# Two transformer blocks: odd attention's norms and scores beside its gate units, modulation blocks in other places of the load stream

## The reference

```
# odd layer: attention of 8 heads of 128, 2 key heads, over keys picked by an indexer
q, k, v, gate, qi, ki, wi = split(norm(x) @ od_w_in)
idx = sum_h wi[h] * relu(qi[h] @ ki.T / 8) + causal       # a row of scores for each query
keep = the 64 largest of each row of idx
logits = (rms(q) * gq) @ (rms(k) * gk).T / sqrt(128) + rel_bias + where(keep, 0, -1e30)
x = x + ((softmax(logits) @ v) * silu(gate)) @ od_w_out

# second block, layer i: six vectors of 1024 out of c, for x and for the context
mod = silu(c) @ ada_w[i] + ada_b[i]                       # 1024 x 6144 for each layer
sh1, sc1, g1, sh2, sc2, g2 = split(mod, 6)
h = rmsnorm(x) * g * (1 + sc1) + sh1
x = x + g1 * attention(h, context)
x = x + g2 * swiglu(rmsnorm(x) * g' * (1 + sc2) + sh2)
```

## Time and profile before

| | us |
|---|---|
| median of 3 runs | 1576.94 |
| lowest, highest | 1575.88, 1579.33 |
| profiled execution | 1575.75 |
| its span in the trace | 1574.0 |
| TensorE busy | 1484.5 (94%) |
| VectorE, ScalarE, GpSimd busy | 734.7, 598.3, 277.4 |
| last input unit of odd attention ends | 286.85 |
| output projection starts, ends | 349.63, 377.5 |

### The profile page before, as it was taken

One profiled execution on the slowest core, in us unless ns is written; L12 is line 12 of the kernel. 1 busy time (PEld: TensorE's weight loads), 2 busy tenths in 40 slices (PEclk: granted clock), 3 DMA queues, 4 the chain that ended last, 5 costly groups with the idle time before them and its releaser, 6 DMA issues.

```text
span 1574.0 us, 22641 instructions
## 1 busy us (share of the span) xinstructions
PE 1484.5 (94%) x9376; PEld 1251.6 (80%) x9376; DVE 734.7 (47%) x1204; ACT 598.3 (38%) x1130; POOL 277.4 (18%) x224
## 2 busy tenths in 40 slices
PE   7899999979999898999999998999999899999997
PEld 6878779847865586888888886688998678899997
DVE  6762145334349744323232234764454773255453
ACT  4434144244337625222122224442343461333342
POOL 2000187002000010211011111244500120021121
PEclk9899999899999998999999999999999999999999
DMA  7412464687200033313232232133351342646450
GB/s 230 164 55 85 160 245 139 252 332 279 81 27 1 28 107 143 125 58 139 85 107 74 95 120 112 54 108 107 114 192 44 107 162 107 267 171 211 168 174 28
DMA packets 36109, 206.84 MB, mean 131 GB/s; under 512 B 4952, under 2 KB 9480, under 8 KB 14888
## 3 DMA queue, kind: packets, MB, share of 16 engines
q1 hardware_dynamic: 33344, 200.11, 35.1%
q10 hardware_dynamic: 1848, 2.52, 0.8%
q0 software_dynamic: 816, 2.78, 0.5%
HBM read 202.76 MB, written 2.62 MB: 130 GB/s over the span
## 4 chain that ended last, share of the span: by engine, by line
PE 84%; DVE 7%; ACT 3%; DMA 3%; issue 1%; POOL 1%; SPq 1%; ACTq 0%; DVEq 0%; POOLq 0%
PE lin L1800 18%; PE lin L1802 17%; PE lin L1801 17%; PE lin L1767 4%; PE lin L1910 4%; PE lin L2381 4%; PE modp L1838 2%; DMA ring<-ada_in 2%; PE lin L2432 1%; PE lin L1783 1%; PE lin L1784 1%; PE lin L1785 1%; PE lin L2160 1%; PE aux L2302 1%; PE aux L1937 1%
## 5 line engine op out<-in xcount | busy, mean ns | idle before, releaser
L620 DVE TENSOR_TENSOR w_split<-ring,w_split 128x1024 fp32r<-128x1024 f32 (+1 forms) x140 | 187.5, 1344 | 358.7 <-ACT w_split L615 358.3
L615 ACT ACTIVATE w_split<-ring 128x1024 fp32r<-128x1024 f32 (+1 forms) x140 | 157.9, 1132 | 413.2 <-PE lin L1802 366.2
L1800 PE MATMUL lin<-hn_hi,w_split 128*128 128x512 f32 (+1 forms) x768 | 266.8, 347 | 3.5 <-DVE w_split L620 3.5
L1802 PE MATMUL lin<-hn_hi,w_split 128*128 128x512 f32 (+1 forms) x768 | 265.4, 346 | 0.0
L1801 PE MATMUL lin<-hn_lo,w_split 128*128 128x512 f32 (+1 forms) x728 | 249.9, 343 | 0.0
L1800 PEld LDWEIGHTS lin<-hn_hi,w_split 128*128 128x128 f32 x768 | 146.2, 190 | 21.1 <-issue 4.1
L1802 PEld LDWEIGHTS lin<-hn_hi,w_split 128*128 128x128 f32 x768 | 146.3, 190 | 17.5
L1801 PEld LDWEIGHTS lin<-hn_lo,w_split 128*128 128x128 f32 x728 | 138.7, 191 | 16.0 <-issue 0.5
L1801 PE MATMUL lin<-hid_split,w_split 128*128 128x512 f32 (+1 forms) x392 | 133.8, 341 | 0.0
L569 POOL TENSOR_TENSOR hn<-hn 128x256 f32<-128x256 f32 (+1 forms) x42 | 43.8, 1042 | 481.1 <-ACT hn L684 480.6
L1800 PE MATMUL lin<-hid_split,w_split 128*128 128x512 f32 (+1 forms) x352 | 118.5, 337 | 2.4 <-POOL hid_split L584 2.4
(11 more groups left out here) (435 smaller groups left out, 2978.7 us busy)
## 6 DMA issues: line engine op xcount, KB each, us to landing
ring<-ada_in SPq DMA_DIRECT2D x48, 1024.0 KB, 5.0
ring<-ssm_in_in SPq DMA_DIRECT2D x24, 1024.0 KB, 4.8
ring<-od_in_in SPq DMA_DIRECT2D x12, 1024.0 KB, 5.0
ring<-ffn0a_in_in SPq DMA_DIRECT2D x11, 1024.0 KB, 4.8
ring<-ffn0b_in_in SPq DMA_DIRECT2D x11, 1024.0 KB, 4.7
ring<-ffn1a_in_in SPq DMA_DIRECT2D x11, 1024.0 KB, 6.3
ring<-ffn1b_in_in SPq DMA_DIRECT2D x11, 1024.0 KB, 4.8
ring<-ev_in_in SPq DMA_DIRECT2D x9, 1024.0 KB, 13.6
```

The lines of the kernel that those rows point to most:

```text
L615: act.activation(parts[:, 0], w, ACT.Copy).then_inc(sig("w_high"), 1)
L620: dve.tensor_tensor(parts[:, 1], w, parts[:, 0].bitcast(F32), ALU.subtract).then_inc(sig("w_low"), 1)
L1800: mm(lin[0:m, tile % RING, 0:width], hi, x_hi, start=kt == 0, stop=False)
L1802: ins = mm(lin[0:m, tile % RING, 0:width], lo, x_hi, start=False, stop=kt == kts - 1)
```

## The change

The load stream is reordered: blocks 4 to 10 of the modulation go between the input blocks, 11 to 19 follow them, 20 to 23 come behind the output blocks and 24 to 27 between the query blocks. TensorE's calls follow. Head sums, row spreads, value transposes and scores go into passes 8, 9 and 10 of the input loop; the head squares, their root and the value copy go into ScalarE's loop over the gate tiles; VectorE forms the reciprocals and adds groups 0 and 1 inside the top-k search and applies the norms before the two adds of the biases. Groups 2 to 6 are added to `mod` in the query stage.

```diff
@@ -56,9 +56,13 @@
 STREAM = [
-    ("ev_in", 9, 2 * KT * P), ("glu", 2, 4 * 4 * P), ("ev_out", 4, 2 * KT * P), ("ada", 4, 2 * KT * P),
-    ("od_small", 1, KT * SMALL), ("od_in", 12, 2 * KT * P), ("ada", 20, 2 * KT * P), ("od_out", 2, 2 * KT * P),
-    ("qkv", 2, 2 * KT * P), ("od_out", 2, 2 * KT * P), ("ada", 4, 2 * KT * P), ("qkv", 4, 2 * KT * P), ("w_o", 4, 2 * KT * P),
+    ("ev_in", 9, 2 * KT * P), ("glu", 2, 4 * 4 * P), ("ev_out", 4, 2 * KT * P), ("ada", 4, 2 * KT * P), ("od_small", 1, KT * SMALL),
+    ("od_in", 2, 2 * KT * P), ("ada", 1, 2 * KT * P), ("od_in", 2, 2 * KT * P), ("ada", 1, 2 * KT * P),
+    ("od_in", 2, 2 * KT * P), ("ada", 1, 2 * KT * P), ("od_in", 2, 2 * KT * P), ("ada", 1, 2 * KT * P),
+    ("od_in", 2, 2 * KT * P), ("ada", 1, 2 * KT * P), ("od_in", 1, 2 * KT * P), ("ada", 2, 2 * KT * P),
+    ("od_in", 1, 2 * KT * P), ("ada", 9, 2 * KT * P), ("od_out", 2, 2 * KT * P), ("qkv", 2, 2 * KT * P),
+    ("od_out", 2, 2 * KT * P), ("ada", 4, 2 * KT * P), ("qkv", 2, 2 * KT * P), ("ada", 2, 2 * KT * P),
+    ("qkv", 1, 2 * KT * P), ("ada", 2, 2 * KT * P), ("qkv", 1, 2 * KT * P), ("w_o", 4, 2 * KT * P),
     ("ffn0a_in", 2, 2 * KT * P), ("ada", 4, 2 * KT * P), ("ffn0a_in", FH - 2, 2 * KT * P),
...
     ("ssm_dt", 1, KT * 2 * M_HEADS), ("ssm_in", 1, 2 * KT * P), ("ada", 2, 2 * KT * P), ("ssm_in", 23, 2 * KT * P),
@@ -777,7 +781,7 @@
             for u in range(W_UNITS):
...
             act.wait_ge(sig("ctx_in"), 16)
-            act_norm(act, 2, 2 * L, "od_out", (0, 0, 0), True, later=6)
+            act_norm(act, 2, 2 * L, "od_out", (0, 0, 0), True, later=5)
             def exps(i, j):
                 act.wait_ge(sig("maxima2"), 3 * i + j + 1)
@@ -806,6 +810,8 @@
                     weights_hi(act, "qkv", n + W_UNITS)
...
                 frees(act.activation(dst, lin[:, tile % RING, :], ACT.Copy), "lin", tile)
+                if n == 6:
+                    ada_copies(act, 6, 1)
                 if n == 5:
...
                            lambda n_: v_tok2[:, 2 * n_:2 * n_ + 2, :].rearrange("p a b -> p (a b)"))
@@ -1163,10 +1169,10 @@
                     dve.tensor_copy(mask_b2, mask2).then_inc(sig("masks2"), 1)
...
                     rope(0)
-                    modulations(dve, own, 6, 1)
                 if u == 10:
...
             rope(2)
+            modulations(dve, own, 2, 5)
             for j in range(3):
...
             shares(0, 0)
@@ -1478,17 +1484,21 @@
                     if m >= 2:
...
                     frees(act.activation(rel[:, m % 2], aux[:, tile % AUX], ACT.Relu, scale=64 ** -0.5), "aux", tile)
-            taken(act, "lin", lin_of["od_in"] + 23)
-            own.mark(act.activation(sq1[:, 0:2, :], k1, ACT.Square))
-            act.activation(sq1[:, 2:10, :], q1, ACT.Square).then_inc(sig("squares_qk1"), 1)
-            ada_copies(act, 1, 1)
-            roots(act, "kq_norm1", 20, 1.0 / P)
-            copies(act, "v_tok1", 1, lambda ps: ps, lambda n: v_tok1.rearrange("p a b -> p (a b)"))
-            ada_copies(act, 2, 2)
+                if n == 16:
+                    taken(act, "lin", lin_of["od_in"] + 15)
+                    own.mark(act.activation(sq1[:, 0:2, :], k1, ACT.Square))
+                    act.activation(sq1[:, 2:10, :], q1, ACT.Square).then_inc(sig("squares_qk1"), 1)
+                if n == 17:
+                    ada_copies(act, 1, 1)
+                if n == 18:
+                    roots(act, "kq_norm1", 20, 1.0 / P)
+                if n == 20:
+                    copies(act, "v_tok1", 1, lambda ps: ps, lambda n_: v_tok1.rearrange("p a b -> p (a b)"))
+            ada_copies(act, 2, 1)
             softmax_exps(act, own, 1, (lh0, lh1), small, False)
+            ada_copies(act, 3, 1)
+            copies(act, "probs1", OD_HEADS, lambda ps: ps[:, 0:3 * P], lambda h: pt1[:, h, :])
             ada_copies(act, 4, 1)
-            copies(act, "probs1", OD_HEADS, lambda ps: ps[:, 0:3 * P], lambda h: pt1[:, h, :])
-            ada_copies(act, 5, 1)
             second_block_scalar(act, own)
         @block.vector
@@ -1711,14 +1721,16 @@
                 for qt, width in ((0, P), (1, L)):
...
                 own.settle()
+                if r == TOPK // 16:
+                    inverses(dve, "kq_norm1", 20)
+                    modulations(dve, own, 0, 2)
             for qt, width in ((0, P), (1, L)):
                 own.mark(ts(sel[:, qt, 0:width], idx[:, qt, 0:width], TAKEN / 2, NEG, ALU.is_gt, ALU.mult))
+            over_roots(dve, "kq_norm1", [(k1[:, n], qk_g[:, 3:4]) for n in range(2)] +
+                       [(q1[:, n], qk_g[:, 2:3]) for n in range(8)])
             own.settle()
...
             own.mark(tt(lh1, bias_b, sel[:, 1, :].unsqueeze(1).to_broadcast([P, OD_HEADS, L]), ALU.add))
-            inverses(dve, "kq_norm1", 20)
-            over_roots(dve, "kq_norm1", [(k1[:, n], qk_g[:, 3:4]) for n in range(2)] +
-                       [(q1[:, n], qk_g[:, 2:3]) for n in range(8)])
             own.settle()
...
             probabilities(dve, own, 1, (lh0, lh1), small, False)
@@ -1726,7 +1738,6 @@
                 tile = aux_of["out1"] + n
...
                 frees(tt(q1[:, n, :], aux[:, tile % AUX, 0:L], gate1[:, n, :], ALU.mult), "aux", tile)
-            modulations(dve, own, 0, 6)
...
                 if n % 2 == 0 and n < 4:
@@ -1828,8 +1839,8 @@
                     b = blocks_of["ada"][n]
...
                         pe.wait_ge(sig("silu_c"), 1)
-                    if n in (24, 32, 44):
-                        pe.wait_ge(sig("mod_read"), {24: 1, 32: 3, 44: 4}[n])
+                    if n in (8, 32, 44):
+                        pe.wait_ge(sig("mod_read"), {8: 1, 32: 3, 44: 4}[n])
                     pe.wait_ge(w_in[b % RING], 16 * (b // RING + 1))
...
                         kt = n % 4 * 2 + part
@@ -2074,25 +2085,28 @@
                     split_unit("od_in", m, KT, lambda kt: (od_hi[:, kt, :], od_lo[:, kt, :]), L,
...
                 between(n)
-            ada(4)
-            ada_groups(1)
-            pe.wait_ge(sig("squares_qk1"), 1)
-            head_sums("kq_norm1", [[n] for n in range(10)], 1, lambda n: sq1[:, n, :])
-            ada(2)
-            head_rows("kq_norm1", 10, 1)
-            tokens("v_tok1", lambda n: v1[:, n], 2)
-            ada(2)
+                if n in (1, 3, 5, 7):
+                    ada(1)
+                if n == 8:
+                    ada_groups(1)
+                    pe.wait_ge(sig("squares_qk1"), 1)
+                    head_sums("kq_norm1", [[m] for m in range(10)], 1, lambda m: sq1[:, m, :])
+                if n == 9:
+                    head_rows("kq_norm1", 10, 1)
+                    tokens("v_tok1", lambda m: v1[:, m], 2)
+                    ada(1)
+                if n == 10:
+                    for m in range(5):
+                        taken(pe, "aux", aux_of["over_kq_norm1"] + m)
+                    scores(1, lambda h, qt: q1[:, h, qt * P:(qt + 1) * P], lambda h: k1[:, h // 4, :])
+                    ada(2)
+            ada(1)
             ada_groups(2)
-            for n in range(5):
-                taken(pe, "aux", aux_of["over_kq_norm1"] + n)
-            scores(1, lambda h, qt: q1[:, h, qt * P:(qt + 1) * P], lambda h: k1[:, h // 4, :])
             ada(4)
             ada_groups(3)
+            transposed_probs(1, (lh0, lh1))
             ada(4)
             ada_groups(4)
-            transposed_probs(1, (lh0, lh1))
-            ada(4)
-            ada_groups(5)
             for h in range(OD_HEADS):
...
                 begin("aux", tile)
@@ -2173,6 +2187,10 @@
             def attention_begins(u):
                 if u == 3:
+                    ada_groups(5)
+                if u in (3, 5):
+                    ada(2)
+                if u == 7:
                     ada_groups(6)
...
                     pe.wait_ge(sig("at_in"), 48)
```

## The result

The changed kernel takes 1581.61 us (median of 20 runs, 1578.47 to 1587.49) against 1576.90 for the kernel before (20 runs): a ratio of 1.0031, 95% interval 1.0021 to 1.0040, or 4.7 us more. The profiled execution took 1580.86 us with a span of 1579.0. The prediction said 1579.8 us, with a range of its own from 1577 to 1583.

What follows compares the result with a forecast made beforehand. TensorE was taken as the bound, with idleness before the output projection and none in the query stage. A gain of 1.3 us and a cost of 4.2 made +2.9, 1579.8 us from the median; own range 1577 to 1583, whole range 1572 to 1585.

Steps and rivals of the forecast that it cites:

- Step 1: Before modulation group 1's sums: TensorE waits about 2.5 us for ScalarE's copy, which stands behind a late weight half.
- Step 2: Head sums in the input loop: 7.1 us as before, ending at the low clock; units 18 and 19 lose 2.2 us.
- Step 3: Scores in the input loop: after two tiles TensorE waits 2.1 us for the bank that ScalarE's value copy frees.
- Step 4: Before the transposes: softmax late behind ScalarE's last gate and group 2's copy; 4.9 us of idleness replace the 6.4.
- Step 5: Transposes to output projection: low clock loses 2.3 us; projection starts at 348.3 instead of 349.63, a gain of 1.3 us.
- Step 6: Query units: blocks 24 to 27, one more group sum and two switches add 4.2 us, with no idleness to hide them.
- The sum: Whole kernel: -1.3 before the projection and +4.2 in the query units make +2.9 us, 1579.8 from the median.
- 3.6 us of blocks have left the stretch: Stretch before the output projection: it gains only 1.3 us although 3.6 us of modulation blocks leave it.
- (a): Slower rival, 1584.3: clock stays low from before the transposes through four blocks, losing 6.8 us, not 2.3; chance 0.18.
- (b): Faster rival, 1572: head sums between dense units and the transposes keep the upper clock, -7.8 us; chance 0.12.
- (c): Much faster rival, 1568: the stretch's 9.7 us of idleness go because ScalarE reaches the softmax early; chance 0.08.
- (d): No-change rival, 1577: loads land in time before group sums and scores, so some 3 us of waits fall away; chance 0.12.

Runs made afterwards that it cites:

- query blocks alone: Kernel before with only modulation blocks 24 to 27 and their group sum moved into the query units: 1577.16 against 1579.15 us, ratio 0.9996.
- copies first: Changed kernel with ScalarE's group 1 and value copies moved ahead of weight halves that wait for loads: 1575.73 against 1579.15 us for the kernel before, ratio 0.9988.
- tail mended: Changed kernel with those two copies early, exponentials before the last two gates, block 9 before the scores, transposes between later blocks: 1575.90 us, ratio 0.9991 to kernel before.
- copies first, again: Repeat of the changed kernel with the two ScalarE copies early: 1575.86 against 1577.57 us for the kernel before, ratio 0.9984.

## Why the prediction was right, point by point

- **Step 1 (wait of 2.5 us before the group sums).** Measured 2.11 and 2.21, released by ScalarE's copy, behind a half, a Silu table and a gate as listed. The experiment that takes the copy away from behind them removes the wait. Shown.
- **Step 2 (7.1 us for the sums, 2.2 for units 18 and 19).** Sums 6.69 and 6.57; the units took 281.52 to 289.93, 8.4 us against 8.0. The low clock lasted 10.2 us as in the earlier trace rows.
- **Step 3 (2.1 us inside the scores).** Measured 1.72 and 3.37. Confirmed in cause, and removed with the early value copy.
- **Step 4 (1.5 + 3.5 + 1.4 us).** The step's three waits make 6.4 us; its "4.9 in place of the 6.4" leaves out the first of them, though the count of time has it. Measured in the first trace: 4.6 (3.18 + 0.50 + 0.92). The part that failed is the split: "Then it waits for ScalarE's copy of group 3 ... until 62.4". TensorE waited for block 15 instead, 3.18 us against 1.5, and the softmax ran under that wait. I had let block 15's load take the 5.0 us of an undisturbed one; after the 7.5 idle us of DMA, blocks 12 to 15 were asked for close together, and the nine blocks issued from 296 to 336 us took 7.6 us to land (median). The same view of the kernel before has almost the same figure (second line), so the trace that the prediction had could have given it; the 5.0 us were those of the input blocks.

```profile
ring<-ada_in SPq DMA_DIRECT2D x9, 1024.0 KB, 7.6
ring<-ada_in SPq DMA_DIRECT2D x12, 1024.0 KB, 7.7
```

  In the second trace both came: 2.27 for DMA and 1.96 for the copy, 5.5 in all with the 1.28 of VectorE. That the step's total came near, 4.6 and 5.5 for 6.4, is in part luck: too little for DMA stood beside too much for the copy. The exponentials' order is the smaller part: moved, they brought 1 or 2 us at most.
- **Step 5 (projection at 348.3, 1.3 us earlier).** 2.6 us earlier in one trace and 0.8 later in the other (143.1 less the 142.3 of before), 1.0 earlier by the means of both pairs. Transposes lost 2.2 us against 2.3.
- **Step 6 (4.2 us in the query units).** 4.5: without a low-clock spell at their start 63.2 us (query blocks alone and copies first, as both traces of the kernel after have the spell) against 58.7, with one 64.8 against 60.3. Of the 0.3 more, 0.23 are two pairs of 1.93 for four blocks of 3.63.
- **The sum (+2.9).** Measured 4.7, in the forecast's own range, but beyond the 3.2 us below which it saw no difference; the chance given to slower by more than that was 0.43. The difference of 1.8 us has two parts that the traces show: 0.3 in step 6, and a spell at the start of the query units worth 1.6 us, which the only trace of before that the prediction had lacked, and the second one had. Both traces of after have it, one of the two of before; how often each kernel has it is open, so the rest is not settled. The two parts make 1.9, but the medians and two traces cannot be split to 0.1 us; that they fit so well is luck.
- **Why "3.6 us of blocks have left the stretch" brought only 1.** Alone they bring 7.0 in one trace. The other part of the change, norms and scores beside the gates, therefore costs some 6 us in the stretch (7.0 less the mean gain of 1.0; by the ratios of the times, 1.0031 against 0.9996, it is 5.5), and 5.1 and 6.2 of them come back with the two copies (134.6 and 136.9 against 139.7 and 143.1). The prediction had those waits, but measured them against the waits of before, and not the gain of four loads that came off a DMA-bound tail.
- **The rivals.** (a) the clock did not stay low through the four blocks (3.83 us against 3.63). Its condition, a wait of more than about 2.4 us, is not what decides: in tail mended a spell begins at 330 us behind waits of 1.35 and 1.44. (b) did not come: the sums took 6.69 us and the transposes 5.38 at the low clock, and dense units without a wait ahead of the sums did not prevent it either (6.98 us in copies first, again). (c) did not come, as step 4's order held ScalarE back. (d) fell with the waits of steps 1 and 3. The drain behind a table load that the Trainium skill states (ScalarE: Activation LUTs, "What ACT_TABLE_LOAD costs") does not show in this trace: the gate starts at 273.79, 0.01 us behind the load that ends at 273.78.

## What to carry to other kernels

An engine that runs in order and also converts weights as they land is a queue of the loads: before work is moved beside such a loop, put every small copy that another engine will want ahead of the next conversion that needs a load. Price a weight block where it stands, by its load (2.5 us) in a stretch that runs ahead of its queue, by its matmuls (0.91 us) where the queue is ahead; moving it gains at most the first and pays the second (here four blocks gained 7.0 us in a trace and cost 4.5). Take the time of a load from blocks that queue in the same way (7.7 us here), not from undisturbed ones (5.0). Where a single trace carries a term of the clock, take a second trace of the same kernel first: here its spells moved one stage by 2 us between two of an unchanged one.

## What the runs showed that I had not expected

- The granted clock's low spells are not a property of a kernel alone: the same kernel had two from 270 to 410 us in one profiled execution (1575.75 us) and four in the other (1579.72 us). They go with the spread of the times: among 29 executions of the kernel before on one chip the shortest, 1573.67 us, has a mean clock of 0.975 and the longest, 1584.90 us, one of 0.967.
- VectorE's reciprocal of 768 columns took 4.95 us, 6.4 ns a column, where a product of 2048 columns takes 2.29 us, 1.1 ns a column.
- A spell need not follow an idle stretch. In copies first, again, the one-column sums start at 273.63 directly behind units and group sums, with no idle piece, and the clock falls at 275.5. Once low, the clock stayed low over work without a gap: in the kernel after it is 0.50 from 277.20 to 287.30, over the last 4.5 us of the sums and most of units 18 and 19, with TensorE busy in 10.10 of 10.10 us.
